# Second mixer's list reordered around its attention units, splits moved from GpSimd to VectorE, own PSUM banks for the first feed-forward unit

## What is computed

```python
proj = jnp.einsum('bsd,dk->bsk', h, w_in)
h_cq, h_ckv, h_kr, h_moba, h_dil, h_gate = jnp.split(proj, [i0, i1, i2, i3, i4], axis=-1)
a = mla_attention(h_cq, h_ckv, h_kr, q_norm, w_uq, kv_norm, w_ukv)      # 6 heads from a low-rank latent
b = moba_attention(mqkv[0], mqkv[1], mqkv[2], slopes[DIL_HEADS:])       # 6 heads
c = ...                                       # 12 heads in 3 dilation groups, joined by their log-sums
gates = jax.nn.sigmoid(h_gate).reshape(B, S, N_BRANCHES, D_MODEL)
merged = (gates[:, :, 0] * jnp.einsum('bsk,kd->bsd', a, w_br_mla)
          + gates[:, :, 1] * jnp.einsum('bsk,kd->bsd', b, w_br_moba)
          + gates[:, :, 2] * jnp.einsum('bsk,kd->bsd', c, w_br_dil))
return jnp.einsum('bsd,de->bse', merged, w_out)
```

## Time and profile before

| | us |
|---|---|
| median of 3 runs | 2845.95 |
| lowest, highest | 2844.62, 2849.30 |
| profiled execution, its own time | 2850.33 |
| its span, first to last instruction | 2848.5 |
| TensorE busy | 2753.6 |
| VectorE busy | 1581.8 |
| ScalarE busy | 1383.3 |
| GpSimd busy | 127.7 |

### The profile page before, as it was taken

The page is one execution under the profiler, slowest core; times in us unless marked ns, Lnnn a source line. Parts: engine busy times, 40 slices in busy tenths (PEclk is TensorE's granted clock), DMA queues, the critical chain, the costliest instruction groups (busy, mean ns, idle before and its releaser), DMA issues.

```text
span 2848.5 us, 40924 instructions
## 1 busy us (share of the span) xinstructions
PE 2753.6 (97%) x16656; PEld 2425.9 (85%) x16656; DVE 1581.8 (56%) x1690; ACT 1383.3 (49%) x1520; POOL 127.7 (4%) x150
## 2 busy tenths in 40 slices
PE   6999999999999999999999999998999999998999
PEld 5889899978888898998888889887888889888787
DVE  4546754655554675456545455556545445466544
ACT  4445664454544566644445444444445444544443
POOL 0000060000000003300000000001000000001000
PEclk9999999999999999999999999999999999999999
DMA  6555445465565553545555555434555555433653
GB/s 205 185 187 168 147 141 160 133 202 190 178 198 187 161 161 115 170 136 174 188 192 184 192 182 172 133 104 141 192 191 184 190 191 166 136 116 104 199 188 129
DMA packets 396950, 475.15 MB, mean 167 GB/s; under 512 B 26950, under 2 KB 365198, under 8 KB 396558
## 3 DMA queue, kind: packets, MB, share of 16 engines
q1 hardware_dynamic: 391776, 470.79, 52.1%
q10 hardware_dynamic: 5038, 2.40, 0.3%
HBM read 467.51 MB, written 5.64 MB: 166 GB/s over the span
## 4 chain that ended last, share of the span: by engine, by line
PE 87%; ACT 5%; DVE 4%; issue 1%; DVEq 1%; DMA 0%; ACTq 0%; SPq 0%
PE bank L322 27%; PE bank L324 26%; PE bank L323 26%; ACT w_hi L311 2%; PE bank L629 1%; DVE w_lo L317 1%; PE bank L1879 1%; PE bank L443 1%; PE bank L1857 1%; PE bank L1173 1%; DVE w_lo L722 1%; PE bank L1149 1%; PE bank L1867 1%; PE bank L1856 1%; DMA raw<-in_ffn_w_in 0%
## 5 line engine op out<-in xcount | busy, mean ns | idle before, releaser
L722 DVE TENSOR_TENSOR w_lo<-raw,w_hi 128x2048 fp32r<-128x2048 f32 x240 | 550.1, 2292 | 530.3 <-ACT w_hi L693 530.3
L322 PE MATMUL bank<-w_hi,xn_hi 128*128 128x512 f32 (+3 forms) x2240 | 806.0, 360 | 13.5 <-DVE hidden L727 9.5
L324 PE MATMUL bank<-w_hi,xn_lo 128*128 128x512 f32 (+3 forms) x2240 | 798.8, 357 | 0.0
L323 PE MATMUL bank<-w_lo,xn_hi 128*128 128x512 f32 (+3 forms) x2240 | 798.7, 357 | 0.0
L693 ACT ACTIVATE w_hi<-raw 128x2048 fp32r<-128x2048 f32 x240 | 459.0, 1913 | 409.8 <-PE bank L324 409.8
L317 DVE TENSOR_TENSOR w_lo<-raw,w_hi 128x2048 fp32r<-128x2048 f32 (+1 forms) x198 | 436.3, 2205 | 314.3 <-ACT w_hi L311 313.7
L322 PEld LDWEIGHTS bank<-w_hi,xn_hi 128*128 128x128 f32 x2240 | 425.9, 190 | 79.3 <-DVE w_lo L722 12.6
L324 PEld LDWEIGHTS bank<-w_hi,xn_lo 128*128 128x128 f32 x2240 | 426.0, 190 | 60.6
L323 PEld LDWEIGHTS bank<-w_lo,xn_hi 128*128 128x128 f32 x2240 | 426.3, 190 | 58.8
L311 ACT ACTIVATE w_hi<-raw 128x2048 fp32r<-128x2048 f32 (+1 forms) x202 | 369.4, 1829 | 86.6 <-PE bank L324 86.6
L322 PE MATMUL bank<-xn_hi,w_hi 128*128 128x256 f32 x1376 | 401.7, 292 | 0.0
(11 more groups left out here) (317 smaller groups left out, 2715.5 us busy)
## 6 DMA issues: line engine op xcount, KB each, us to landing
raw<-in_w_in SPq DMA_DIRECT2D x126, 1024.0 KB, 5.2
raw<-in_ffn_w_in SPq DMA_DIRECT2D x176, 512.0 KB, 4.7
raw<-in_ffn_w_out SPq DMA_DIRECT2D x44, 1024.0 KB, 4.9
raw<-in_ffn_w_gate SPq DMA_DIRECT2D x88, 512.0 KB, 4.0
raw<-in_ffn_w_up SPq DMA_DIRECT2D x88, 512.0 KB, 4.9
raw<-in_ffn_w_down SPq DMA_DIRECT2D x44, 1024.0 KB, 4.9
raw<-in_w_out SPq DMA_DIRECT2D x10, 1024.0 KB, 4.8
raw<-in_w_branch_b SPq DMA_DIRECT2D x8, 1024.0 KB, 5.2
```

What stands on the lines that cost most here:

```text
L322: pe.matmul(out, a_hi, b_hi, start=start, stop=False, skip_group_check=check)
L323: pe.matmul(out, a_hi, b_lo, start=False, stop=False, skip_group_check=check)
L324: return pe.matmul(out, a_lo, b_hi, start=False, stop=stop, skip_group_check=check)
L722: dve.tensor_tensor(w_lo[slot][:, :], raw[slot][:, :], w_hi[slot][:, :].bitcast(F32), ALU.subtract).then_inc(s_lo, 1)
```

## The change

1. **List.** In `MIX2` the three `mob` items go ahead of the latents, and `up` ahead of the last two `dv` items. The units move two items forward, to 6 to 11, 16 to 21 and 22 to 25. The latents' norm moves with them to item 8 (its sums now in bank 5), their split to item 10. As the roots now fall between the exponentials of two units, ScalarE's program has two more table loads in each second mixer.
2. **Sigmoids.** Those of pairs 0 and 1 are taken in the last two items of the list, those of 2 and 3 behind them.
3. **GpSimd** makes no lower parts any more. VectorE makes one behind each pair.
4. **After a mixer** (`q % 3 == 2`) VectorE makes the lower part of the next item 0 behind two updates of x instead of ahead of them.
5. **Feed-forward.** Unit 0 accumulates in banks 6 and 7, so unit 1 does not wait for `hidden` of unit 0.

```diff
-MIX2 = ([("mv", 1184), ("mv2", 1440), ("cq", 0), ("ckv", 256)] + [("mob", 416 + 256 * i) for i in range(3)]
-        + [("dil", 1568 + 256 * i) for i in range(6)] + [("dv", 3104 + 256 * i) for i in range(3)] + [("up", 0)]
+MIX2 = ([("mv", 1184), ("mv2", 1440)] + [("mob", 416 + 256 * i) for i in range(3)] + [("cq", 0), ("ckv", 256)]
+        + [("dil", 1568 + 256 * i) for i in range(6)] + [("dv", 3104), ("up", 0), ("dv", 3360), ("dv", 3616)]
...
         def to_ffn_dve(dve, q, p, update):
-            split_lo(dve, p, 0)
+            late = q % 3 == 2
+            if not late:
+                split_lo(dve, p, 0)
             for c in range(4):
                 update(dve, q, c, BY_HALVES)
                 gain_dve(dve, q, c, BY_HALVES)
                 if c == 1:
+                    if late:
+                        split_lo(dve, p, 0)
                     low_dve(dve, q, 0, BY_HALVES)
...
+        def gate_bank(u):
+
+            return 6 if isinstance(u, int) and u == 0 else 4
...
                 if first:
                     pe.wait_ge(s_xlo, 4 * q + (2 * h + t + 1))
-                elif h == 0:
+                elif h == 0 and not (isinstance(u, int) and u == 1):
                     pe.wait_ge(s_hid[t], f * UNITS + u)
...
-                units.append((8 + h, [(mob[lo:lo + 64, h // 2, :], mob[lo:lo + 64, 3 + h // 2, :], 384 + 64 * h,
+                units.append((6 + h, [(mob[lo:lo + 64, h // 2, :], mob[lo:lo + 64, 3 + h // 2, :], 384 + 64 * h,
...
-                if j == 5:
+                if j == CKV + 2:
                     dve.wait_ge(s_lroot, l + 1)
                     dve.reciprocal(linv[:, :, :], lroot[:, :, :])
...
+                if j >= N2 - 2:
+                    sigmoid_act(act, j - (N2 - 2))
             out2_act(act, po, l)
...
+                if j == 0:
+                    pe.wait_ge(s_L, l * 8 + 8)
                 for b, ((hi, lo), k0, k) in enumerate(outs):
-                    if j == 0 and b == 2:
-                        values_pe(pe, l, 15)
-                        pe.wait_ge(s_L, l * 8 + 8)
...
             split_hi(act, po, 1)
-            out_hi_act(act, l, 15)
-            act.drain()
-            sigmoid(0)
             split_hi(act, po, 2)
-            for j in range(1, 4):
-                sigmoid(j)
+            for j in range(2, 4):
+                sigmoid_act(act, j)
...
-                if j >= 2:
-                    if j == 2:
-                        dve.wait_ge(s_lo, po.base + (5 + START))
-                    split_lo(dve, po, j + 3)
+                split_lo(dve, po, j + 3)
...
-            for l in range(LAYERS):
-                po = in_layer(plans[1], 2, l)
-                pool.wait_ge(s_lo, po.base + (3 + START))
-                split_lo(pool, po, 3)
-                split_lo(pool, po, 4)
```

More of the change, by code:

```diff
@@ L608, in gate_up @@
                 for k in range(4):
-                    mm = product(pe, bank[4 + t][:, :], xn_hi[:, 4 * h + k, tok(t)], xn_lo[:, 4 * h + k, tok(t)],
+                    mm = product(pe, bank[(6 if first else 4) + t][:, :], xn_hi[:, 4 * h + k, tok(t)], xn_lo[:, 4 * h + k, tok(t)],
                                  hi[:, k, :], lo[:, k, :], h == 0 and k == 0, h == 1 and k == 3)
@@ L726, in hide @@
                 dve.wait_ge(s_gact, (f * UNITS + u) * 2 + (t + 1))
-                dve.scalar_tensor_tensor(out=hidden[:, t, :], in0=bank[4 + t][:, 256:512], scalar=rstd[:, t:t + 1],
+                dve.scalar_tensor_tensor(out=hidden[:, t, :], in0=bank[gate_bank(u) + t][:, 256:512], scalar=rstd[:, t:t + 1],
                                          in1=gate_act[:, t, :], op0=ALU.mult, op1=ALU.mult).then_inc(s_hid[t], 1)
@@ L1795, in build @@
         N2 = len(MIX2)
-        UP = 16
+        KINDS2 = [k for k, _ in MIX2]
+        MOB0, CKV, DIL0, UP, GATE0 = (KINDS2.index(k) for k in ("mob", "ckv", "dil", "up", "gate"))
+        DV = [j for j, k in enumerate(KINDS2) if k == "dv"]
         def unit_plan():
@@ L2052, in mixer2_act @@
                         n = 128 if kind == "mv2" else 256
-                        at = {"mv": 384, "mv2": 640}.get(kind, 768 + 256 * (j - 13))
+                        at = {"mv": 384, "mv2": 640}[kind] if kind != "dv" else 768 + 256 * DV.index(j)
                         ins = act.activation(v2[:, :, at:at + n], b[:, :, 0:n], ACT.Copy)
                     else:
-                        t = 2 * (j - UP - 1)
+                        t = 2 * (j - GATE0)
                         ins = act.activation(gates2[:, t:t + 2, :], b, ACT.Copy)
@@ L2115, in mixer2_dve @@
                     ins.then_inc(s_lat, 1)
-                if j == 7:
+                if j == CKV + 4:
                     dve.wait_ge(s_lhi, l + 1)
@@ L2137, in out2_pe, with sigmoid_act @@
             return out_pe(pe, po, 4, s2_mlo, l * 4, (2, 2, 2, 1, 1))
+        def sigmoid_act(act, j):
+            gate = gates2[:, :, :].rearrange("p (i k) t -> p i (k t)", i=3)[:, :, 2 * T * j:2 * T * j + 2 * T]
+            act.drain()
+            act.activation(gate, gate, ACT.Sigmoid).then_inc(s2_gate, 1)
         def out2_act(act, po, l):
-            def sigmoid(j):
-                gate = gates2[:, :, :].rearrange("p (i k) t -> p i (k t)", i=3)[:, :, 2 * T * j:2 * T * j + 2 * T]
-                act.activation(gate, gate, ACT.Sigmoid).then_inc(s2_gate, 1)
             split_hi(act, po, 1)
-            out_hi_act(act, l, 15)
-            act.drain()
-            sigmoid(0)
             split_hi(act, po, 2)
-            for j in range(1, 4):
-                sigmoid(j)
+            for j in range(2, 4):
+                sigmoid_act(act, j)
             for j in range(6):
@@ L2159, in out2_dve @@
             split_lo(dve, po, 1)
-            out_lo_dve(dve, l, 15)
             split_lo(dve, po, 2)
```

22 lines of the change are left out of this document (11 added, 11 removed).

## The result

The changed kernel took 2822.77 us (median of four, 2813.22 to 2824.99) beside 2847.62 for the kernel before: ratio 0.9906, 95% interval 0.9881 to 0.9932. The forecast was 2819 in 2811 to 2829. In two later measurements the same kernel came out at 2816.33 (ratio 0.9896, 0.9882 to 0.9910) and 2816.23 (0.9892, 0.9870 to 0.9914). Over the executions of this study it is a mean of 2818.5 us (13 of them) against 2849.2 (55, without the four behind the 2847.62, whose clocks are not on record): 30.7 us, 1.1%. The runs of the experiments were spread over three chips. Beside them the kernel before took 2848.2, 2849.2 and 2848.5 us in the mean (18, 14 and 15 executions), so the chip hardly matters here. But eight more executions of it on the third chip gave a mean of 2853.1, four of them near 2858 at a mean clock of 0.988: a mean of few executions can be off by 4 us through the clock alone.

What follows compares the result with a forecast made beforehand. TensorE, busy 97% of the span, was taken as the bound, so only waits and slow clock could move. 9.5 + 2.4 + 16.2 = 28.1 us, less 1 for the clock, gave 27.1 and 2819 us, range 2811 to 2829.

Steps and rivals of the forecast that it cites:

- (a): Feed-forward parts, first unit in banks 6 and 7: the waits for `hidden` go, 9.5 us gained, no bound below 8.
- (b): Four hand-offs from mixer to feed-forward, low part behind two updates of x: 0.6 us gained each, 2.4 in four.
- (f): Rest of the list: nothing else moves; DMA has the same loads in another order, the queue three items ahead.
- (c): Way out of the second mixers, splits off GpSimd: VectorE takes 6.92 us a pair, TensorE 5.76; waiting depends on head start.
- (d): Tail of the list and way out: new waits of 2.15 and 0.8 us a layer in place of 22.1 in two; gain 16.2.
- (e): Latent norm moved from item 5 to 8: unit 3's maximum 2.2 us late, cost 0, other bound 2.2 a layer.
- R5: Slower: VectorE's 2.2 us lag after item 8 never heals, TensorE waits in 13 units a layer, 2876 us; chance 0.03.
- The clock: Way out of the second mixers: 6.1 us lost to slow clock beyond the waits in two layers, counted as gained.
- 1 us given back: Start of the way out: 1 us taken off the gain because the clock may fall after the new 2.15 us waits.
- R1: Way out keeps its slow clock and each layer waits 2 us longer: 10 us more, 2829 us; chance 0.15.
- R3: More than forecast: way out does not wait at all, TensorE's clock also higher in the first mixers, 2812 us; chance 0.10.

Runs made afterwards that it cites:

- e1: Only the first feed-forward unit's banks changed (6 and 7), in the kernel before: median 2838.7 us, ratio 0.9969.
- e3: The changed kernel with the feed-forward parts of before, so only the list and way out of the second mixers changed: median 2839.8 us, ratio 0.9973.
- e4: The changed kernel with GpSimd again making the lower parts of way-out items 3 and 4: median 2832.74 us, ratio 0.9940.
- e8: The changed kernel with the reciprocal of the latents' norm executed twice: median 2829.28 us, ratio 0.9926.
- e6: The changed kernel with pair 0's sigmoid one item earlier and pair 1's behind the upper parts of way-out items 1 and 2: medians 2820.03 and 2816.70 us.

## Why the prediction was right, and where not

*(a)* 9.5 forecast. In e1 the eight waits went, 9.3 us in the mean. Right.

*(b)* 0.6 each forecast, 0.85 measured on the old list (a wait of 0.85 where 1.2 was forecast). What the step did not see is the coupling. It took the load of item 0 for in time, and (f) said "the same loads in another order". On the new list the load lands late, and without (b), as in e3, each of the two hand-offs behind the second mixers waits 3.3 us. There (b) is worth 2.4 us, and a forecast for the list alone would have been 3 us too good for that.

*(c)* The sequence of 6.92 us a pair was exact, and it is what brings `merged` to 0.16 and 0.62 us. e4 confirms that GpSimd was the cause, at a higher price.

*(d)* Forecast 2.15 and 0.8 a layer; measured 2.22 and 2.23 at the start, 0.16 and 0.62 before the output projection: 5.2 in two layers where 5.9 was forecast. TensorE starts the output projection at 1942.58, 32.9 us after the end of the last gate item but one, where 32.0 was forecast. The 0.8 came smaller in every layer of the three profiles: 0 to 0.5 where TensorE itself was slow behind the first wait, 0.3 to 0.6 where it was not.

*(e)* The maximum of unit 3 started 3.3 us after its item's end and the next one 1.5: 1.9 us late, healed after one unit, no wait. Forecast 2.2 late and 0. e8 puts the spare time at 0.9 us, the `o_mob` that the step names, not the 3.6 of the transposition. R5 falls: a lag of 5.3 us healed as well. The rows of the changed kernel:

```profile
1752.20 3.35 DVE L2121 RECIPROCAL latent_inv<-latent_root 128x512 f32<-128x512 f32 x1
...
1756.83 0.42 DVE L1917 TENSOR_TENSOR o_mob<-bank,o_mob 128x256 fp32r<-128x256 f32 x1
1757.16 0.55 DVE L1926 SCALAR_TENSOR_TENSOR scores<-consts,bank 128x384 f32<-128x384 f32 x1
...
1758.17 0.65 PE L1889 MATMUL bank<-probs_t,values 128*64 128x256 f32 x2
```

*The clock.* The sum had 6.1 us of slow clock in the way out, less 1 given back: 5.1. Other executions of the kernel before lose more than the one profiled (10.4 us in the way out of the second profile against 8.6, both with 1.8 or 1.9 inside waits). The "1 us given back" was somewhat small: in three profiles of the changed kernel the clock fell behind three of six such waits, some 1.7 us each, 1.7 an execution. In all, the clock gave some 6.4 us. R1 did not come. Whether a part of R3 did, less loss in the first mixers, is not shown: 8.6 to 8.8 us against 15.6 before, but other kernels with the same first mixers lost up to 20.6.

*The time.* The forecast was 27.1 us less, 22.0 by waits and 5.1 by the clock. Measured were 30.7 in the mean (24.9 in the medians of the first four executions), 24.3 by waits and some 6.4 by the clock. Both parts were put a little too low, and the mechanism of each holds. That 2819 lies so near the mean of 2818.5 is luck: the forecast set out from a median of 2845.95, 3.3 us below the mean of the kernel before, and its gain was 3.6 us too small; the two errors cancel. The waits, 23.6 against 22.0 in the rows that the change touches, are the number that tests the reasoning.

## What to carry over

Price an edit with the neighbours it will have: the lower part moved behind two updates looked like 0.85 us on the old kernel and is worth 2.4 behind the new way out, because the faster way out makes a load late that had been in time. Where VectorE's instructions have two SBUF operands, as here, taking GpSimd's long elementwise work from beside them can pay even though VectorE then has more to do, and its fixed period of 6.92 us was easy to forecast from. And compare variants by waits as well as by time, but keep slow clock inside a wait apart: 2.8 us less waiting in the way out (e6) did not show in a time that moves by 4 us with the clock.

## What was unexpected in the hardware

- The length of a wait did not decide by itself whether TensorE's clock fell. Behind the 2.2 us wait at the start of the way out it fell in 8 of 12 cases (changed kernel, e3, e4, e8) and stayed at 1.00 in the others. Behind the 0.5 us waits at the three-headed units, six in each of 13 profiles, it fell in 17 of 78. "TensorE: Matmul & The Clock Gate" of the Trainium skill, section "HAM oscillation — how this bites in real kernels", ties the falls to long idle gaps; these rows differ, and they decide here. The section behind it, "A second HAM failure mode: psum-queue depth-cycling", has falls from frequent short idle moments, which is nearer to these rows.
- The same program lost 8.6 to 20.6 us by the clock in its first mixers, while its largest difference in waits there was some 2 us (`sb_qT`: 4.1 to 6.0). No run here says what sets this.
- A VectorE sum with two SBUF inputs was held to the end of a GpSimd operation twice in a row (4.91 and 4.43 us for 0.69), while products that read a bank took 1.87 while GpSimd was at work (kernel before) and 1.88 while it was not.
